# A gated network's gate and up products as seven half-size block products

## The chip, the core and the metric

The kernel runs on one NeuronCore of a Trainium2 chip. The core has a matrix engine (TensorE, "PE" in the profile; its weight loads are the row "PEld"), VectorE ("DVE"), ScalarE ("ACT"), GpSimd ("POOL") and SyncE ("SP"), which issues the transfers here. Each engine runs its own instructions in order and waits on semaphores for the others. The metric is the device time of one execution, in microseconds.

## What is computed

A sequence of 512 tokens of 1,024 values passes through a first block (a convolution and attention mixer, an attention to a memory, a feed-forward network with a short convolution) and then two layers of a second one. Each of the two layers has two gated networks, called here f10, f20 (layer 0) and f11, f21 (layer 1). Between f10 and f20 stands a pooling mixer, between f11 and f21 an attention with latent projections. The change touches the four gated networks alone.

```python
def swiglu(h, w_gate, w_up, w_down):
    return (jax.nn.silu(h @ w_gate) * (h @ w_up)) @ w_down
...
        h = rmsnorm_2(x, ffn1_norm[i])
        x = x + FFN_HALF * swiglu(h, ffn1_w_gate[i], ffn1_w_up[i], ffn1_w_down[i])
```

Here `w_gate` and `w_up` are 1024x2816 and `w_down` is 2816x1024. All is float32.

## The kernel before

**Numbers in two parts.** A float32 product is made of three matmuls in a rounded format (`fp32r`): every operand is split into a high part (rounded) and a low part (the rest), and `mm3` (L386 to L388) issues high by high, low by high and high by low. So each block of weights, once it has come by a transfer into a slot `raw`, is rounded into `wh` by ScalarE (`high`, L370), and VectorE subtracts that from the original into `wl` (`low`, L378). The stream x stands with its channels on the partitions, x[:, k, :] for the eight blocks k of 128 channels; its scaled halves are `hxh` (ScalarE, L515) and `hxl` (VectorE, L523).

**A unit** is one block of weights that makes one output tile of 128x512: eight row blocks of 128x128 (128x1024 in the profile) for gate and up, and for down eight, eight and six (the last is 128x768). A gated network has 22 tiles c. For each, `swiglu_tensor` (L1604) computes a gate tile and an up tile, 24 matmuls of 512 columns each. The first two units are run as a pair, k by k, since the last blocks of x come late. VectorE multiplies both tiles by the row factor `rs` of the norm (L1647, L1652), ScalarE takes the silu (L1637), GpSimd multiplies the two (L1703), ScalarE rounds the product into `hh` (L1640) and GpSimd makes its low part `hl` (L1705). All 22 are kept. Then each of the eight output tiles m takes three units of down, 66 matmuls, after which VectorE adds half of the result to x[:, m, :] (L1692), ScalarE splits and squares it for the next stage (L515, L447), VectorE makes `hxl` (L523), and GpSimd adds up the squares (L452).

**What sets the order** is the order in which the functions of each engine are written: nothing is scheduled by a tool. `swiglu_scalar` and `swiglu_vector` convert the weights two units ahead. `raw`, `wh` and `wl` have three slots each; a transfer into `raw` waits for the `low` three units earlier, a `high` for the matmuls three units earlier. The factor `rs` is made while the first tiles are computed: TensorE adds up the squares (L461), VectorE turns them into a mean square (L477), GpSimd takes the inverse root (L484), TensorE spreads it (L494) and ScalarE keeps it (L501). In f10 the spreading stands one unit later in TensorE's order than in the others (`LATE`).

## Time and profile before

| | |
|---|---|
| median of three runs | 2551.04 us (2550.62 to 2552.26) |
| profiled execution, span | 2550.8 us |
| TensorE (PE) busy | 2514.7 us, 99% |
| VectorE (DVE) busy | 1215.6 us, 48% |
| ScalarE (ACT) busy | 933.4 us, 37% |
| GpSimd (POOL) busy | 622.4 us, 24% |
| chain of work that ended last | 89% TensorE, 6% VectorE |

The page gives for each engine the time in which it had work. Matmuls overlap each other: a row's duration (0.39 us at 512 columns) is a latency, and the distance between the starts of two rows is what one costs. A row of VectorE that says "x2" covers two instructions, one after the other. What stands in brackets behind a row is how long the engine sat idle before it, and what ended that. "PEclk" is TensorE's granted clock as a share of its full 2.4 GHz.

### The profile page before, as it was taken

What the parts mean: (1) busy time and instruction counts of PE and PEld (TensorE: products, weight loads), DVE (VectorE), ACT (ScalarE), POOL (GpSimd) and SP (SyncE); (2) the same over time, 40 slices, a digit from 0 to 9 for tenths busy, and PEclk for the clock granted to TensorE, in tenths of its full rate; (3) what the DMA queues carried; (4) which work ended last, traced back from release to release, by engine and by line L of the source; (5) the groups of instructions that cost most, each with busy time, mean ns of one, the idle gap of its engine ahead of it and who ended that gap; (6) DMA issues with size and microseconds to landing.
All of it is one profiled execution on the core that took longest, in us unless ns stands there. A gap on an engine that the chain in (4) does not pass through costs nothing.

```text
span 2550.8 us, 28691 instructions
## 1 busy us (share of the span) xinstructions
PE 2514.7 (99%) x11642; PEld 2073.3 (81%) x11642; DVE 1215.6 (48%) x1607; ACT 933.4 (37%) x1371; POOL 622.4 (24%) x477
## 2 busy tenths in 40 slices
PE   8999999999999999999999999999999999999999
PEld 7777777888887888888888888888888888888887
DVE  5896655565635333335333333333336566433322
ACT  4486443444323332224333222332223554433221
POOL 3673403222203222101222101222101431322200
PEclk9999999999999999999999999999999999999999
DMA  5211312323232233332323332323332111333232
GB/s 171 71 46 58 105 44 67 107 92 98 93 99 81 90 93 98 98 97 75 107 92 96 96 99 88 108 93 97 92 100 87 42 50 58 94 96 95 93 99 93
DMA packets 66483, 227.26 MB, mean 89 GB/s; under 512 B 7216, under 2 KB 8752, under 8 KB 66352
## 3 DMA queue, kind: packets, MB, share of 16 engines
q1 hardware_dynamic: 66352, 225.44, 28.1%
q8 instruction: 92, 1.51, 0.3%
q14 instruction: 39, 0.32, 0.0%
HBM read 223.31 MB, written 2.10 MB: 88 GB/s over the span
## 4 chain that ended last, share of the span: by engine, by line
PE 89%; DVE 6%; ACT 2%; issue 1%; POOL 1%; DMA 0%; SPq 0%; DVEq 0%; ACTq 0%; POOLq 0%
PE main L386 19%; PE main L388 19%; PE main L387 19%; PE score L386 7%; PE score L388 6%; PE score L387 6%; PE out L386 3%; PE out L388 3%; PE out L387 3%; DVE wl L378 1%; DVE hxl L523 1%; DVE tmp L1347 1%; PE main L2055 1%; ACT wh L370 0%; PE turn L1027 0%
## 5 line engine op out<-in xcount | busy, mean ns | idle before, releaser
L378 DVE TENSOR_TENSOR wl<-raw,wh 128x1024 fp32r<-128x1024 f32 (+1 forms) x431 | 562.8, 1308 | 806.9 <-ACT wh L370 805.9
L370 ACT ACTIVATE wh<-raw 128x1024 fp32r<-128x1024 f32 (+1 forms) x431 | 439.9, 1024 | 635.7 <-PE main L388 473.2
L386 PE MATMUL main<-hxh,wh 128*128 128x512 f32 x1200 | 470.9, 392 | 8.2 <-DVE tmp L687 4.2
L388 PE MATMUL main<-hxh,wl 128*128 128x512 f32 x1200 | 467.9, 390 | 0.0
L387 PE MATMUL main<-hxl,wh 128*128 128x512 f32 x1200 | 467.8, 390 | 0.0
L386 PE MATMUL main<-hh,wh 128*128 128x512 f32 x880 | 342.4, 389 | 0.5 <-DVE wl L378 0.5
L387 PE MATMUL main<-hl,wh 128*128 128x512 f32 x880 | 342.3, 389 | 0.0
L388 PE MATMUL main<-hh,wl 128*128 128x512 f32 x880 | 342.3, 389 | 0.0
L452 POOL TENSOR_TENSOR acc<-acc,sq 128x512 f32<-128x512 f32 (+1 forms) x88 | 128.2, 1456 | 617.4 <-ACT sq L447 612.1
L386 PEld LDWEIGHTS main<-hxh,wh 128*128 128x128 f32 x1200 | 225.7, 188 | 60.1 <-DVE tmp L687 4.3
L388 PEld LDWEIGHTS main<-hxh,wl 128*128 128x128 f32 x1200 | 225.7, 188 | 47.5
L387 PEld LDWEIGHTS main<-hxl,wh 128*128 128x128 f32 x1200 | 225.7, 188 | 45.7
L1703 POOL TENSOR_TENSOR tmp<-tmp,tmp 128x512 f32<-128x512 f32 x88 | 113.5, 1289 | 607.7 <-DVE tmp L1652 562.8
L386 PE MATMUL score<-hxh,wh 128*128 128x512 f32 x656 | 257.3, 392 | 3.0 <-DVE wl L378 1.3
L388 PE MATMUL score<-hxh,wl 128*128 128x512 f32 x656 | 255.4, 389 | 0.0
L387 PE MATMUL score<-hxl,wh 128*128 128x512 f32 x656 | 255.3, 389 | 0.0
L386 PEld LDWEIGHTS main<-hh,wh 128*128 128x128 f32 x880 | 165.2, 188 | 35.0 <-issue 0.9
L387 PEld LDWEIGHTS main<-hl,wh 128*128 128x128 f32 x880 | 165.2, 188 | 34.4
L388 PEld LDWEIGHTS main<-hh,wl 128*128 128x128 f32 x880 | 165.2, 188 | 34.2
L1640 ACT ACTIVATE hh<-tmp 128x512 fp32r<-128x512 f32 x88 | 55.7, 633 | 317.8 <-POOL tmp L1703 317.8
L386 PEld LDWEIGHTS score<-hxh,wh 128*128 128x128 f32 x656 | 123.2, 188 | 32.3 <-DVE hxl L523 4.0
L388 PEld LDWEIGHTS score<-hxh,wl 128*128 128x128 f32 x656 | 123.1, 188 | 25.9
(434 smaller groups left out, 3412.5 us busy)
## 6 DMA issues: line engine op xcount, KB each, us to landing
raw<-in_wts SPq DMA_DIRECT2D x375, 512.0 KB, 3.5
raw<-in_wts SPq DMA_DIRECT2D x52, 384.0 KB, 3.0
x<-in_xT SPq DMA_DIRECT2D x4, 512.0 KB, 8.3
out<-x SPq DMA_DIRECT2D x8, 256.0 KB, 3.2
memx<-in_memT SPq DMA_DIRECT2D x1, 1024.0 KB, 9.6
raw<-in_wts SPq DMA_DIRECT2D x4, 256.0 KB, 2.6
band<-in_pool SPq DMA_DIRECT2D x1, 768.0 KB, 4.2
rope<-in_rope SPq DMA_DIRECT2D x1, 512.0 KB, 7.1
```

Of the source, the lines that this page charges most:

```text
L370: e.activation(wh[i % NCONV][:, 0:n], raw[i % NRAW][:, 0:n], ACT.Copy).then_inc(*sig.up("weight_high", ("high", i)))
L378: e.tensor_tensor(wl[i % NCONV][:, 0:n], raw[i % NRAW][:, 0:n], f(wh[i % NCONV][:, 0:n]), ALU.subtract) \
L386: e.matmul(o, ah, bh, start=start, stop=False)
L387: e.matmul(o, ah, bl, start=False, stop=False)
L388: return e.matmul(o, al, bh, start=False, stop=stop)
L452: e.tensor_tensor(acc[:, 0:n], acc[:, 0:n], sq_turn(nm).of(("sq", nm, k))[:, 0:n], ALU.add) \
L523: e.scalar_tensor_tensor(hxl[:, k, :], x[:, k, :], col(gain, k), f(hxh[:, k, :]), ALU.mult, ALU.subtract) \
L1347: e.scalar_tensor_tensor(s[:, :], y[:, m, :], col(gain, m), turnb.of(("rows", nm))[:, :], ALU.mult, ALU.mult) \
L1640: e.activation(hh[:, c, :], s[:, :], ACT.Copy).then_inc(*sig.up("h_high", ("hh", nm, c)))
L1703: e.tensor_tensor(s1[:, :], s1[:, :], s2[:, :], ALU.mult).then_inc(*sig.up("h_joined", ("joined", nm, c), ("free", (nm, "us", c))))
L2055: made = e.matmul(o[:, n * i:n * i + n], s[:, i * P:(i + 1) * P], ones[:, 2:4] if halves else ones[:, 0:1], start=True, stop=True)
```

## The change

Each gated network now runs in three rounds of 8, 8 and 6 tiles (`ROUNDS_OF`). In a round the tiles are computed and at once multiplied by their rows of down, for all eight m; the results are added into x three times over, each scaled by `rs` (so the up tiles are no longer scaled), and the part of the product that is kept (`bh`, `bl`) has eight tiles in place of 22.

Of the 22 tiles, 15 are computed as **blocks**: for a tile c, gate and up are taken as a matrix of 2x2 blocks (gate and up; upper and lower half of the 1,024 rows), and the stream as one of 2x2 blocks (upper and lower half of the rows; left and right 256 tokens). The eight products of blocks are replaced by seven, `UP_LEFT`, `UP_RIGHT`, `S1` to `S4` and `GATE_RIGHT`, some of them of sums of blocks. One product is 4 row blocks by 3 matmuls by 256 columns. The sums of weights (`sum_step`, four of 128x512 a tile) and the recombination (`up_left_vector` and the functions after it) are VectorE's; the sums of the stream (`turned_sums_vector`, four blocks k, once a network) are VectorE's too, with ScalarE rounding them. ScalarE copies three intermediate results out of the accumulating bank (`keep_scalar`). The other seven tiles stay plain: three at the start (`OPENING`) as before, and four (`HALVED`) in units of half the rows.

Conversions are now of halves (128x512), up to six halves ahead of TensorE, sums nine halves ahead, and during the down units four halves (two units) ahead. `raw`, `wh` and `wl` get a fourth slot in these networks. GpSimd makes only the low part of each gated tile (`h_low`); the multiplication goes to VectorE. The core of the diff:

```diff
+NHALF = 6
+HALF = 512
+AHEAD = 6
+Q = 256
...
+ROUNDS_OF = ((0, 8), (8, 8), (16, 6))
+BLOCKED = ("f10", "f20", "f11", "f21")
+OPENING = 3
+HALVED = (5, 10, 13, 18)
+UP_LEFT, UP_RIGHT, S4, GATE_RIGHT, S1, S2, S3 = 1, 2, 3, 4, 5, 6, 7
+GATE_TOP, GATE_LOW, UP_TOP, UP_LOW = 8, 9, 10, 11
+GATE, UP = 12, 13
+SUMS = (S1, S2, S3, S4)
+
...
+def tile_order(rnd):
+
+    c0, n = ROUNDS_OF[rnd]
+    order, behind = [], []
+    for c in range(c0, c0 + n):
+        if c < OPENING:
+            order += [(c, GATE), (c, UP)]
+        elif c in HALVED:
+            order += [(c, GATE_TOP), *behind[:1], (c, GATE_LOW), *behind[1:], (c, UP_TOP), (c, UP_LOW)]
+            behind = []
+        else:
+            order += [(c, UP_LEFT), (c, UP_RIGHT), *behind[:1], (c, S2), *behind[1:], (c, S1), (c, S3)]
+            behind = [(c, GATE_RIGHT), (c, S4)]
+    return order + behind
 
 
...
+            src, ready = weight_source(i)
+            e.wait_ge(*sig.at(ready))
+            for old in held[i]:
+                e.wait_ge(*sig.at(("unit", old)))
+            if half_at[i] >= NHALF:
+                e.wait_ge(*sig.at(area_ready[stage_name(units[i][0])]))
+            e.activation(halves_of(wh, i), src, ACT.Copy).then_inc(*sig.up("weight_high", ("high", i)))
...
+            if which == S1:
+                a, b, op = raw_half(r + 1, 0), raw_half(r + 1, 1), ALU.add
+            elif which == S2:
+                e.wait_ge(*sig.at(("summed", tile, S1)))
+                a, b, op = sums.of(("sum", tile, S1))[:, :], raw_half(r, 0), ALU.subtract
+            elif which == S3:
+                a, b, op = raw_half(r, 0), raw_half(r + 1, 0), ALU.subtract
+            else:
+                e.wait_ge(*sig.at(("summed", tile, S2)))
+                a, b, op = raw_half(r, 1), sums.of(("sum", tile, S2))[:, :], ALU.subtract
+            e.tensor_tensor(t[:, :], a, b, op).then_inc(*sig.up("weights_summed", ("summed", tile, which)))
+
...
+        def weights_ahead(step, e, i, halves=AHEAD):
+            for n in range(i + 1, reach(i, halves) + 1):
+                step(e, n)
...
+            first = which in (UP_LEFT, UP_RIGHT, S1)
+            e.wait_ge(*sig.at(("low", i)))
+            for k in range(4):
+                mh, ml, ready = moving(nm, which, k)
+                e.wait_ge(*sig.at(ready))
+                e.matmul(b[:, LEFT], h[:, k, :], mh, start=first and k == 0, stop=False, skip_group_check=not first)
+                e.matmul(b[:, LEFT], h[:, k, :], ml, start=False, stop=False, skip_group_check=not first)
+                made = e.matmul(b[:, LEFT], lo[:, k, :], mh, start=False, stop=k == 3, skip_group_check=not first)
+            made.then_inc(*sig.up("unit_done", ("unit", i)))
...
+        def down_step(e, nm, rnd, m, ks):
+            c0, n = ROUNDS_OF[rnd]
+            i = down_unit(nm, rnd, m)
+            b, (h, lo) = down_banks.of((nm, "bank", rnd, m)), weights_of(i)
+            e.wait_ge(*sig.at(("low", i)))
+            for k in ks:
+                e.wait_ge(*sig.at(("h", nm, c0 + k)))
+                made = mm3(e, b[:, :], (h[:, k, :], lo[:, k, :]), (bh[:, k, :], bl[:, k, :]), k == 0, k == n - 1)
+                if k == n - 1:
+                    made.then_inc(*sig.up("unit_done", ("unit", i)))
...
+                for m in range(2):
+                    _, old = down_banks.take((nm, "bank", rnd, m))
+                    e.wait_ge(*sig.at(old))
+                    down_step(e, nm, rnd, m, range(0, 2))
+                    block_product(e, nm, c0 + n - 1, (GATE_RIGHT, S4)[m])
+                for m in range(2):
+                    down_step(e, nm, rnd, m, range(2, n - 1))
+                for m in range(2):
+                    down_step(e, nm, rnd, m, range(n - 1, n))
+                for m in range(2, KC):
+                    _, old = down_banks.take((nm, "bank", rnd, m))
+                    e.wait_ge(*sig.at(old))
+                    down_step(e, nm, rnd, m, range(n))
+            wide.pass_over(2 * FT + (3 if nm == "f11" else 0))
...
+            e.activation(tsum[:, k, 3 * Q:4 * Q], x[:, k, LEFT], ACT.Copy, scale=col(GAIN[nm], k)).then_inc(*sig.up("left_kept", ("x left", nm, k)))
...
+            g, n = col(GAIN[nm], 4 + k), (slice(0, Q), slice(Q, 2 * Q), slice(2 * Q, 3 * Q), slice(3 * Q, 4 * Q))
+            e.wait_ge(*sig.at(("x left", nm, k)))
+            e.scalar_tensor_tensor(tsum[:, k, n[0]], x[:, k, RIGHT], col(GAIN[nm], k), tsum[:, k, n[3]], ALU.mult, ALU.subtract) \
+                .then_inc(*sig.up("turned_sum", ("t1 sum", nm, k)))
+            e.wait_ge(*sig.at(("t1 sum", nm, k)))
+            e.scalar_tensor_tensor(tsum[:, k, n[1]], x[:, 4 + k, RIGHT], g, tsum[:, k, n[0]], ALU.mult, ALU.subtract) \
+                .then_inc(*sig.up("turned_sum", ("t2 sum", nm, k)))
+            e.wait_ge(*sig.at(("t2 sum", nm, k)))
+            e.tensor_tensor(tsum[:, k, n[3]], tsum[:, k, n[1]], tsum[:, k, n[3]], ALU.subtract).then_inc(*sig.up("turned_sum"))
+            e.scalar_tensor_tensor(tsum[:, k, n[2]], x[:, 4 + k, LEFT], g, tsum[:, k, n[1]], ALU.mult, ALU.subtract) \
+                .then_inc(*sig.up("turned_sum", ("t sum", nm, k)))
...
+        def keep_scalar(e, nm, c, which):
+            t, old = kept_turn.take((nm, "kept", c, which))
+            e.wait_ge(*sig.at(old))
+            e.wait_ge(*sig.at(("unit", part_no[(nm, c), which])))
+            e.activation(t[:, :], a_banks.of((nm, "a", c))[:, LEFT], ACT.Copy).then_inc(*sig.up("sum_kept", ("kept", nm, c, which)))
...
+        def join_blocks(e, nm, c):
+            g = tile_turn.of((nm, "gate", c))
+            e.wait_ge(*sig.at(("silu", nm, c)))
+            e.wait_ge(*sig.at(("up", nm, c)))
+            e.tensor_tensor(g[:, :], g[:, :], tile_turn.of((nm, "up", c))[:, :], ALU.mult) \
+                .then_inc(*sig.up("blocks_joined", ("joined", nm, c), ("free", (nm, "up", c))))
...
+        def h_low(e, nm, c):
+            e.wait_ge(*sig.at(("hh", nm, c)))
+            e.tensor_tensor(bl[:, c % 8, :], tile_turn.of((nm, "gate", c))[:, :], f(bh[:, c % 8, :]), ALU.subtract) \
+                .then_inc(*sig.up("gated_low", ("h", nm, c), ("free", (nm, "gate", c))))
...
+                        weights_ahead(sum_weights, e, part_of(nm, c, which), AHEAD + 3)
+                        weights_ahead(low, e, part_of(nm, c, which))
+                    if rnd == 0 and s == 0:
+                        turned_sums_vector(e, nm, 0)
+                        turned_sums_vector(e, nm, 1)
+                        turned_low_vector(e, nm, 0)
+                    if rnd == 0 and s == (3 if nm in LATE else 2):
+                        mean_square(e, nm, 1.0 / D)
+                    if rnd == 0 and 2 <= s < 5:
+                        if s < 4:
+                            turned_sums_vector(e, nm, s)
+                        turned_low_vector(e, nm, s - 1)
+                    if rnd == 0 and s == 5:
+                        gate_plain_vector(e, nm, 0)
+                        gate_plain_vector(e, nm, 1)
+                    if rnd == 0 and s == 6:
+                        gate_plain_vector(e, nm, 2)
...
+                    weights_ahead(sum_weights, e, down_unit(nm, rnd, m), AHEAD)
+                    weights_ahead(low, e, down_unit(nm, rnd, m), 4)
+                    y, old = tile_turn.take((nm, "y", rnd, m))
+                    e.wait_ge(*sig.at(old))
+                    e.wait_ge(*sig.at(("unit", down_unit(nm, rnd, m))))
+                    e.scalar_tensor_tensor(y[:, :], down_banks.of((nm, "bank", rnd, m))[:, :], 0.5, rs[:, :], ALU.mult, ALU.mult) \
+                        .then_inc(*sig.up("y_scaled", ("y", nm, rnd, m), ("free", (nm, "bank", rnd, m)), *([("free", ("rs", nm))] if (rnd, m) == (2, KC - 1) else [])))
+                    e.wait_ge(*sig.at(("y", nm, rnd, m)))
+                    e.tensor_tensor(x[:, m, :], x[:, m, :], y[:, :], ALU.add) \
+                        .then_inc(*sig.up("x_even", ("x", nm, m) if rnd == 2 else ("x", nm, rnd, m), ("free", (nm, "y", rnd, m))))
+                    if rnd == 2 and next_nm:
+                        split_low(e, next_nm, m, next_gain)
+
...
-            for m in range(KC):
-                for p in range(3):
-                    low(e, u + 2 * FT + 3 * m + p + 2)
-                e.wait_ge(*sig.at(("unit", u + 2 * FT + 3 * m + 2)))
-                e.scalar_tensor_tensor(x[:, m, :], mainb.of(("y", nm, m))[:, :], 0.5, x[:, m, :], ALU.mult, ALU.add) \
-                    .then_inc(*sig.up("x_even", ("x", nm, m), ("free", ("y", nm, m))))
-                if next_nm:
-                    split_low(e, next_nm, m, next_gain)
...
-                s1, s2 = half_turn.of((nm, "gs", c)), half_turn.of((nm, "us", c))
-                e.wait_ge(*sig.at(("silu", nm, c)))
-                e.wait_ge(*sig.at(("up", nm, c)))
-                e.tensor_tensor(s1[:, :], s1[:, :], s2[:, :], ALU.mult).then_inc(*sig.up("h_joined", ("joined", nm, c), ("free", (nm, "us", c))))
-                e.wait_ge(*sig.at(("hh", nm, c)))
-                e.tensor_tensor(hl[:, c, :], s1[:, :], f(hh[:, c, :]), ALU.subtract).then_inc(*sig.up("h_low", ("h", nm, c), ("free", (nm, "gs", c))))
```

**TensorE, inside tile 8 of f20.** Before, the end of a gate unit and the start of the up unit (`main`, `score`, `out` are banks of results; behind the arrow stand the stream's part and the weights' part):

```order
L386 MATMUL score<-hxh_53,wh_59 128x512
L387 MATMUL score<-hxl_54,wh_59 128x512
L388 MATMUL score<-hxh_53,wl_62 128x512
L386 MATMUL score<-hxh_53,wh_60 128x512 [waits s_weight_low,s_half_scaled]
L387 MATMUL score<-hxl_54,wh_60 128x512
L388 MATMUL score<-hxh_53,wl_63 128x512
```

After, the end of `UP_RIGHT` and the start of `S2` (`th`, `tl` are the parts of the stream's sums):

```order
L1853 MATMUL out<-hxh_53,wh_60 128x256
L1854 MATMUL out<-hxl_54,wh_60 128x256
L1855 MATMUL out<-hxh_53,wl_63 128x256
L1853 MATMUL main<-th_144,wh_142 128x256 [waits s_weight_low,s_sum_kept]
L1854 MATMUL main<-tl_145,wh_142 128x256
L1855 MATMUL main<-th_144,wl_143 128x256
```

The matmuls have half as many columns, and `S2` waits for the copy that ScalarE makes of the bank after `UP_LEFT`.

**VectorE, output tiles of the last down round of f20.** Before, two output tiles m, three units of weights each:

```order
L1692 SCALAR_TENSOR_TENSOR x_49<-main,x_49 128x512 [waits s_unit_done]
L523 SCALAR_TENSOR_TENSOR hxl_54<-x_49,colsb_64,hxh_53 128x512 [waits s_x_high]
L378 TENSOR_TENSOR wl_63<-raw_57,wh_60 128x768 [waits s_weight_high]
L378 TENSOR_TENSOR wl_61<-raw_55,wh_58 128x1024 [waits s_weight_high]
L378 TENSOR_TENSOR wl_62<-raw_56,wh_59 128x1024 [waits s_weight_high]
L1692 SCALAR_TENSOR_TENSOR x_49<-main,x_49 128x512 [waits s_unit_done]
L523 SCALAR_TENSOR_TENSOR hxl_54<-x_49,colsb_64,hxh_53 128x512 [waits s_x_high]
L378 TENSOR_TENSOR wl_63<-raw_57,wh_60 128x768 [waits s_weight_high]
L378 TENSOR_TENSOR wl_61<-raw_55,wh_58 128x1024 [waits s_weight_high]
L378 TENSOR_TENSOR wl_62<-raw_56,wh_59 128x1024 [waits s_weight_high]
```

After, again two output tiles, one unit each:

```order
L2117 SCALAR_TENSOR_TENSOR tmp_77<-score,rs_69 128x512 [waits s_unit_done,s_gated_low]
L2120 TENSOR_TENSOR x_49<-x_49,tmp_77 128x512 [waits s_y_scaled]
L716 SCALAR_TENSOR_TENSOR hxl_54<-x_49,colsb_64,hxh_53 128x512 [waits s_x_high]
L526 TENSOR_TENSOR wl_62<-raw_57,wh_59 128x768 [waits s_weight_high]
L2117 SCALAR_TENSOR_TENSOR tmp_78<-out,rs_69 128x512 [waits s_unit_done,s_blocks_joined]
L2120 TENSOR_TENSOR x_49<-x_49,tmp_78 128x512 [waits s_y_scaled]
L716 SCALAR_TENSOR_TENSOR hxl_54<-x_49,colsb_64,hxh_53 128x512 [waits s_x_high]
L526 TENSOR_TENSOR wl_63<-raw_141,wh_60 128x768 [waits s_weight_high]
```

Per output tile one instruction came in ahead of the addition to x and two conversions went; between two tiles TensorE now has 18 matmuls and not 66.

**VectorE, opening of f10.** Before, from the last `hxl` to the first scaled tiles:

```order
L523 SCALAR_TENSOR_TENSOR hxl_54<-x_49,colsb_64,hxh_53 128x512 [waits s_x_high] x3
L378 TENSOR_TENSOR wl_62<-raw_56,wh_59 128x1024 [waits s_weight_high]
L378 TENSOR_TENSOR wl_63<-raw_57,wh_60 128x1024 [waits s_weight_high]
L378 TENSOR_TENSOR wl_61<-raw_55,wh_58 128x1024 [waits s_weight_high]
L378 TENSOR_TENSOR wl_62<-raw_56,wh_59 128x1024 [waits s_weight_high]
L477 TENSOR_SCALAR stat_51<-turn 128x4 [waits s_sums_done,s_m_divided]
L378 TENSOR_TENSOR wl_63<-raw_57,wh_60 128x1024 [waits s_weight_high]
L1647 TENSOR_TENSOR tmp_74<-score,rs_69 128x512 [waits s_x_even,s_unit_done,s_rows_kept]
L1652 TENSOR_TENSOR tmp_75<-out,rs_69 128x512 [waits s_x_odd,s_unit_done]
```

After, the twelve rows that end with the mean square (two sets of `tsum`, one `tl` and two conversions stand between the last `hxl` and these):

```order
L526 TENSOR_TENSOR wl_61<-raw_55,wh_58 128x1024 [waits s_weight_high]
L552 TENSOR_TENSOR sum_135<-raw_141 128x512 [waits s_unit_done,s_fetched3,s_fetched2]
L552 TENSOR_TENSOR sum_136<-sum_135,raw_57 128x512 [waits s_weights_summed]
L526 TENSOR_TENSOR wl_62<-raw_56,wh_59 128x1024 [waits s_weight_high]
L1943 SCALAR_TENSOR_TENSOR tsum_146<-x_49,colsb_64,tsum_146 128x256 [waits s_left_kept]
L1946 SCALAR_TENSOR_TENSOR tsum_146<-x_49,colsb_64,tsum_146 128x256 [waits s_turned_sum]
L1949 TENSOR_TENSOR tsum_146<-tsum_146 128x256 [waits s_turned_sum]
L1950 SCALAR_TENSOR_TENSOR tsum_146<-x_49,colsb_64,tsum_146 128x256
L1955 TENSOR_TENSOR tl_145<-tsum_146,th_144 128x1024 [waits s_turned_high]
L552 TENSOR_TENSOR sum_137<-raw_57,raw_141 128x512
L526 TENSOR_TENSOR wl_63<-raw_57,wh_60 128x512 [waits s_weight_high] x2
L670 TENSOR_SCALAR stat_51<-turn 128x4 [waits s_sums_done,s_m_divided]
```

The mean square was the fifth instruction after the last group of `hxl`, and now two conversions and sums of the stream and of the weights stand ahead of it.

## Rows read from the trace of the kernel before

**Rows 1.** Page, span; then part 1: busy us (share) xinstructions.

```profile
span 2550.8 us, 28691 instructions
PE 2514.7 (99%) x11642; PEld 2073.3 (81%) x11642; DVE 1215.6 (48%) x1607; ACT 933.4 (37%) x1371; POOL 622.4 (24%) x477
```

**Rows 2.** TensorE's longest wait (start us, us, engine, line), then its stretch (PEclk after POOL).

```profile
61.51 0.56 PE L386 MATMUL main<-hxh,wh 128*128 128x512 f32 x1 [4.21 <-DVE tmp L687]
60.00:73.00 13.00, 11.49 (x44) 9.34 (x45) 11.35 (x15) 3.87 (x5) 2.37 (x2) 0.87 0.26 83
```

**Rows 3.** Timeline, TensorE, 512 columns, first and last of 18 starts.

```profile
1100.10 0.39 PE L386 MATMUL main<-hh,wh 128*128 128x512 f32 x1
...
1103.95 0.39 PE L388 MATMUL main<-hh,wl 128*128 128x512 f32 x1
```

**Rows 4.** Timeline, TensorE, 256 columns, the first and the last of 22 starts.

```profile
129.36 0.28 PE L388 MATMUL main<-mnh,wl 128*128 128x256 f32 x1
...
131.87 0.28 PE L388 MATMUL main<-mnh,wl 128*128 128x256 f32 x1
```

**Rows 5.** Groups by line and form, VectorE: count | busy us, mean ns.

```profile
L1778 DVE SCALAR_TENSOR_TENSOR zl<-main,stat,zh 128x256 fp32r<-128x256 f32 x8 | 3.7, 479 | 1.9 <-ACT zh L1767 1.6
L734 DVE TENSOR_TENSOR mk_l<-main,mk_h 128x256 fp32r<-128x256 f32 x8 | 3.3, 415 | 0.5 <-ACT mk_h L729 0.5
L378 DVE TENSOR_TENSOR wl<-raw,wh 128x512 fp32r<-128x512 f32 x4 | 2.8, 690 | 6.7 <-ACT wh L370 6.7
```

**Rows 6.** Timeline, VectorE, two conversions in a row.

```profile
1173.32 0.69 DVE L1799 TENSOR_TENSOR band_l<-band,band_h 128x512 fp32r<-128x512 f32 x1 [3.47 <-ACT band_h L1791]
1173.93 0.68 DVE L378 TENSOR_TENSOR wl<-raw,wh 128x512 fp32r<-128x512 f32 x1
```

**Rows 7.** As rows 5, ScalarE's and GpSimd's groups.

```profile
L1640 ACT ACTIVATE hh<-tmp 128x512 fp32r<-128x512 f32 x88 | 55.7, 633 | 317.8 <-POOL tmp L1703 317.8
L1705 POOL TENSOR_TENSOR hl<-tmp,hh 128x512 fp32r<-128x512 f32 x88 | 114.4, 1300 | 65.4 <-ACT hh L1640 65.4
```

**Rows 8.** Timeline, VectorE and GpSimd together after 812 us.

```profile
815.19 6.69 DVE L378 TENSOR_TENSOR wl<-raw,wh 128x1024 fp32r<-128x1024 f32 x3
812.88 10.15 POOL L452 TENSOR_TENSOR acc<-acc,sq 128x512 f32<-128x512 f32 x5
```

**Rows 9.** Timeline, opening of f20, VectorE, GpSimd, TensorE.

```profile
1209.64 2.36 DVE L378 TENSOR_TENSOR wl<-raw,wh 128x1024 fp32r<-128x1024 f32 x2 [1.36 <-ACT wh L370]
1215.65 1.02 POOL L484 TENSOR_TENSOR stat<-stat,mhalf 128x4 f32<-128x4 f32 x1 [8.45 <-DVE stat L477]
1220.80 0.60 PE L494 MATMUL turn<-ident,stat 128*128 128x128 f32 x4
```

**Rows 10.** Timeline, last output tile but one of f11, VectorE, ScalarE, GpSimd.

```profile
1904.24 0.69 DVE L1692 SCALAR_TENSOR_TENSOR x<-main,x 128x512 f32<-128x512 f32 x1 [1.70 <-PE main L388]
1905.72 0.75 DVE L523 SCALAR_TENSOR_TENSOR hxl<-x,colsb,hxh 128x512 fp32r<-128x512 f32 x1 [0.79 <-ACT hxh L515]
1906.98 1.47 DVE L378 TENSOR_TENSOR wl<-raw,wh 128x768 fp32r<-128x768 f32 x1 [0.51 <-ACT wh L370]
1904.96 0.72 ACT L515 ACTIVATE hxh<-x,colsb 128x512 fp32r<-128x512 f32 x1 [3.69 <-DVE x L1692]
1905.59 0.62 ACT L447 ACTIVATE sq<-x 128x512 f32<-128x512 f32 x1
1906.11 0.83 ACT L370 ACTIVATE wh<-raw 128x768 fp32r<-128x768 f32 x1
1906.29 1.35 POOL L452 TENSOR_TENSOR acc<-acc,sq 128x512 f32<-128x512 f32 x1 [13.62 <-ACT sq L447]
```

**Rows 11.** Timeline, opening of f10, VectorE and TensorE.

```profile
829.60 0.16 DVE L477 TENSOR_SCALAR stat<-turn 128x4 f32<-128x4 f32 x1 [3.93 <-PE turn L461]
834.92 0.60 PE L494 MATMUL turn<-ident,stat 128*128 128x128 f32 x4
```

**Rows 12.** Timeline, VectorE, the last instruction of the program.

```profile
2548.10 0.69 DVE L1692 SCALAR_TENSOR_TENSOR x<-main,x 128x512 f32<-128x512 f32 x1 [13.06 <-PE main L388]
```

499 lines of the change are left out of this document (376 added, 123 removed).

## The prediction

> **What bounds the kernel now.** I read the page first: TensorE is busy 99% of the span [rows 1], and the longest thing it ever waits for takes 4.2 us [rows 2]. So a change gains what it takes from TensorE's stream and loses what it makes TensorE wait for, and both are counted one by one. Next I read the timeline of TensorE for the distance between starts, since its durations overlap. At 512 columns 17 starts lie in 3.85 us, 226.5 ns each [rows 3]; at 256 columns, in an earlier stage with the same three matmuls and a weight load for each, 21 starts lie in 2.51 us, 119.5 ns each [rows 4]. Half the columns is not half the cost: the difference is 107 ns for 256 columns, which leaves about 12.5 ns for each matmul whatever its size. VectorE is busy 48% over the whole span [rows 1], but it gets most of the new work, so its rows are read by stage.
>
> **What TensorE gains.** 60 tiles (15 in four networks) give up 48 matmuls of 512 columns each, 2,880 in all, and get 84 of 256 columns, 5,040. 2,880 x 0.2265 = 652.3 us, 5,040 x 0.1195 = 602.3 us [rows 3, 4]: a gain of **50.0 us**, 0.84 us a tile (10.87 before, 10.03 after). The down matmuls, 528 a network, stay as they are. The change does what it says: these numbers are the order's own.
>
> A rule of the Trainium skill can be held against this. What the rows show is 12 to 13 ns above the columns' time. The page "TensorE: Matmul & The Clock Gate" (section Back-to-back issue gap) gives columns / 2.4 GHz plus 2.5 ns; by it the change would gain 2,880 x 0.2158 - 5,040 x 0.1092 = 71 us, an estimate from the page. The rows stand against it at both sizes, by 10 ns.
>
> **Steady blocks: can VectorE keep up?** For a block tile it makes four sums and seven conversions of 128x512 and one multiplication, 0.69 us each, and five recombinations of 128x256 at 0.42 us [rows 5]: 12 x 0.69 + 5 x 0.42 = 10.4 us. Two in a row overlap: they start 0.61 us apart, not 0.69 [rows 6], so the tile is about 12 x 0.61 + 5 x 0.34 = 9.0, and 0.2 for steps that need the one before. GpSimd's low part (1.30 us [rows 7]) comes on top, as the two get in each other's way: three conversions of 1024 took 6.69 us beside GpSimd's additions, 2.23 each [rows 8], where two back to back elsewhere took 2.36, 1.2 each [rows 9]. That is 1.0 us for each GpSimd instruction. So 10.3 us stand against TensorE's 10.03. That overrun is small, blocks stand at most three in a row, weights are up to six halves (8.6 us) ahead, and a plain tile (four conversions, two scalings, 3.7 us and GpSimd's 1.0 against 10.87) pays it back. ScalarE has per tile seven conversions and two more of 0.63 and three short copies: under 7 us. I take **0** for the steady part; if the cover goes, see the third rival. The gated tile waits for fewer engines; a round's last one needs about 3.6 us of VectorE, ScalarE and GpSimd after its last product, and has 4.1 us or more of down matmuls ahead of it: 0, bound 1 us a network.
>
> **The last round of down: a new bound.** Before, each output tile m had 66 matmuls (15 us) in which to finish x and split it. Now, in the last round, it has 18: 18 x 0.2265 = 4.08 us. The chain on VectorE for one m can be read from the old one, in the network f11 [rows 10]. From the start of the addition to x (1904.24) over ScalarE's split (1904.96, 0.72), `hxl` (1905.72), ScalarE's square and next conversion (until 1906.94) and GpSimd's addition of squares (until 1907.64), VectorE's next weights are converted at 1906.98 + 1.47 = 1908.45: 4.21 us. All of that is queued in the same order in the new kernel, since VectorE stands at `hxl` until ScalarE has split x, and ScalarE's next `high` stands behind its square. Ahead of it comes the new scaling into y, 0.69 and 0.03 for the hand-over, less 0.08 of overlap. So VectorE needs **4.85 us per m where TensorE needs 4.08**, and it prepares the weights only two units ahead. Followed through: y(0) can start 0.3 after the end of unit 0, which I call 0. The second unit of the next stage is converted seven chains later, two of them with 128x1024 (0.27 longer): 0.3 + 5 x 4.85 + 2 x 5.12 = 34.8. Unhindered, TensorE would reach it at 0.68 (unit 1 ends three matmuls after unit 0) + 6 x 4.08 + 0.68 = 25.8. It waits 9 us. From f20 to f11 and from f11 to the latent stage that is 9.0 each; from f10 to the pooling mixer the next units are smaller, and its chain starts about 8 later, so 8. Together **26 us**; without GpSimd's part (4.4 a chain) 17, and that is the lower bound. f21 has no next stage: its chain is y, x and one conversion, 2.3 us, below 4.08.
>
> At the start of f11 and of the latent stage TensorE then stands still for over 4 us in one piece. The wait of 4.21 us in the trace was followed by a stretch with a mean granted clock of 0.87 [rows 2], that is, 3.4 of 13 us at 1.2 in place of 2.4 GHz, and half of that is lost: 1.7 us. Twice: **3.4 us** (0 to 7).
>
> **Opening of each network.** VectorE now makes the stream's sums there: per block k three of 0.48 and one of 0.42 us [rows 5], about 1.85 with the overlaps and hand-overs, and one conversion of 1.15. Two sets, a conversion, two units and two sums of weights stand ahead of the mean square. In f20, counted from the first conversion of the pair (1209.64 + 1.15): 3.7 + 1.15 + 1.15 + 1.25 + 1.15 gives 1219.2, and with GpSimd's 1.02 the root is there at 1220.4, just before TensorE spreads it (1220.80) [rows 9]. No wait, by 0.4 us. Then two more sets, three `tl`, six halves and three sums, 12.6 us, until the first gate tile is scaled at 1232.5 and its bank free; TensorE wants it at 1221.1 + 10.9 = 1232.0, and the third gate tile's bank 0.9 us later than it is wanted in turn. I take 1.5 to 2 us for f20 and f11 and 1 for f21. f10 is worse: GpSimd's seven additions there run beside VectorE [rows 8], and its mean square stands three conversions later. The sums of the stream last until about 827.5, and then come `tl` (828.7), the third gate unit's conversion (829.9), two sums (831.1), the next conversion (832.3), a set (834.2), `tl` (835.3), a sum and two halves (837.4); the mean square comes at 837.5, not 829.60, and TensorE, which spread it at 834.92 [rows 11], waits until 838.8. With 0.5 for the third gate unit, wanted at 829.4, 1.5 and 0.9 for the banks, 6 us. Together **11 us** (3 to 20).
>
> **The end.** The last x (0.69 us, [rows 12]) gets a scaling ahead of it: **0.7 us**.
>
> **The sum**: -50.0 + 26 + 3.4 + 11 + 0.7 = -8.9 us. The profiled span is 2550.8 us, 0.2 below the median; so 2551.0 - 8.9 = **2542 us**.
>
> **Rivals.** *The gain comes through nearly whole.* The last round's chain stays under 4.08 us, if ScalarE and GpSimd fall between VectorE's instructions otherwise than in [rows 10]; then the 26 and the 3.4 go: 2542 - 29.4 = 2513 us. For it: in the old kernel nothing waited there. Against it: 4.21 us is one unbroken chain of queue order. *The matmuls cost their columns alone.* If the 12.5 ns shrank with the size, 256 columns would take 107 and 512 214 ns: 2,880 x 0.214 - 5,040 x 0.107 = 77 us, so 27 more, 2515 us. Against it: [rows 4], four stretches of that stage alike. By the same page of the Trainium skill the fixed part would be 2.5 ns, which leads nearly there. *VectorE paces the blocks, and it is slower than before.* At whole durations it needs 10.4 + 1.0 = 11.4 us a block tile, 1.4 over TensorE. ScalarE's copy of `UP_LEFT`, for which `S2` waits, stands in its queue behind a conversion whose sum VectorE has yet to make, so some of that reaches TensorE long before the six halves are used up. If a third does, 0.5 us x 60 = 30, and the time is 2572 us. It decides the sign from 8.9 / 60 = 0.15 us a tile on. Against it: the plain tiles between.
>
> **How the numbers follow.** The forecast has a chance of 53%, its own range 2534 to 2553 (17 to 27 for the rounds' ends, 3 to 20 for the openings). The first rival 20% (2505 to 2522), the second 4%, the third 23% (2555 to 2590). From 2518 to 2566 about 8 in 10 are held: half of the first rival and of the second fall below, part of the third above. A measurement of this kernel can tell about 0.2% (5 us) from no change. The forecast's case gives 33 points to faster, 17 to same and 3 to slower; the first two rivals are faster; of the third 3 points are same, 20 slower: faster 57%, same 20%, slower 23%.
>
> **What would show it.** TensorE's starts 119 to 120 ns apart in the blocks; if 129, the gain is gone. In the last round of f20 and f11, VectorE's y operations 4.8 us apart, and TensorE waiting for `wl` up to 9 us in all there, once for over 4. In f10's opening a wait of some 3 us for the root. In the steady blocks no wait over 0.3 us; waits for kept copies or `wl` in every pair would be the third rival. The prediction is wrong in its main term if y stands 4.1 us apart.

## The result, and the profile after

The changed kernel takes 2575.55 us (median of four runs, 2575.05 to 2576.74), the kernel before 2551.65 us beside it. The ratio is 1.0095, with a 95% interval of 1.008 to 1.0109: about 24 us **slower**. I had forecast 2542 us, 9 faster, and the time lies above my range too. The profiled execution has a span of 2574.1 us, 23.3 more than before, so its rows can be set against the old ones directly.

The page, as [rows 1]:

```profile
span 2574.1 us, 34915 instructions
PE 2485.6 (97%) x13802; PEld 2142.7 (83%) x13802; DVE 1743.2 (68%) x2659; ACT 1126.4 (44%) x1915; POOL 529.4 (21%) x389
PE 82%; DVE 11%; ACT 3%; issue 3%; POOL 1%; DMA 1%; SPq 0%; DVEq 0%; ACTq 0%; POOLq 0%
```

TensorE is busy 29 us less than before, although the program is longer: it now stands still. In the chain of work that ended last it has 82% in place of 89%, and VectorE 11% in place of 6%. The view of TensorE's waits (engine, line, tile waited for: us in all, times, the longest) says where:

```profile
PE turn L687 <- POOL stat L677: 10.1, 3, 3.8
PE main L579 <- DVE wl L526: 8.7, 11, 3.5
PE main L579 <- DVE tmp L2117: 8.4, 3, 6.4
PE main L579 <- DVE x L3035: 7.7, 2, 7.4
PE main L579 <- DVE x L2209: 5.3, 1, 5.3
PE turn L662 <- ACT sq L640: 4.9, 1, 4.9
```

Here `stat L677` is the inverse root of a network's norm, `wl L526` a conversion of weights, `tmp L2117` the scaling of a down result into y, `x L3035` and `x L2209` the last additions to x of the attention and of the pooling mixer, and `sq L640` the squares of x ahead of the pooling mixer. None of these was over 0.9 us before. Over the whole program TensorE waits 83 us where it waited 32.

**What the blocks gave.** The distances that answer to [rows 3, 4], in a block tile of f11 (first and last of 20 starts):

```profile
1876.05 0.28 PE L1855 MATMUL main<-th,wl 128*128 128x256 f32 x1
...
1878.33 0.28 PE L1853 MATMUL main<-hxh,wh 128*128 128x256 f32 x1
```

19 distances in 2.28 us are 120.0 ns. The 512-column matmuls stand 226.5 ns apart as before, so the blocks give 2,880 x 0.2265 - 5,040 x 0.120 = 48 us where I had 50. The next lines are windows of f11: its second round from tile 8 to the first down unit, then a block tile alone (length, then busy us of TensorE, weight loads, VectorE, ScalarE, GpSimd; granted clock):

```profile
1707.26:1786.73 79.47, 79.47 (x577) 75.58 (x576) 65.43 (x106) 41.03 (x77) 10.09 (x6) 1.00 0.35 108
1871.49:1881.57 10.08, 10.08 (x86) 10.08 (x85) 8.97 (x17) 5.71 (x12) 0.00 (x0) 1.00 0.28 80
```

TensorE never stops, and the same stretch is 79.47 us long in all four networks. From tile 8 to the last down round nothing is lost anywhere.

**The last down round** (VectorE's and TensorE's timelines in f20; the brackets give the idle time ahead and what ended it):

```profile
1554.04 0.68 DVE L2117 SCALAR_TENSOR_TENSOR tmp<-main,rs 128x512 f32<-128x512 f32 x1
1554.76 0.69 DVE L2120 TENSOR_TENSOR x<-x,tmp 128x512 f32<-128x512 f32 x1
1556.24 0.75 DVE L716 SCALAR_TENSOR_TENSOR hxl<-x,colsb,hxh 128x512 fp32r<-128x512 f32 x1 [0.79 <-ACT hxh L708]
1557.49 1.46 DVE L526 TENSOR_TENSOR wl<-raw,wh 128x768 fp32r<-128x768 f32 x1 [0.50 <-ACT wh L517]
1558.88 0.68 DVE L2117 SCALAR_TENSOR_TENSOR tmp<-score,rs 128x512 f32<-128x512 f32 x1
...
1559.11 0.47 PE L579 MATMUL main<-bh,wh 128*128 128x512 f32 x1 [0.48 <-DVE wl L526]
1563.95 0.47 PE L579 MATMUL main<-bh,wh 128*128 128x512 f32 x1 [0.51 <-DVE wl L526]
...
1574.69 0.76 PE L579 MATMUL main<-hxh,wh 128*128 128x512 f32 x1 [6.41 <-DVE tmp L2117]
```

This is the chain of [rows 10] with the scaling ahead of it: 4.84 us from y to y. TensorE follows at that pace, and stands still 6.4 us before f11. Its waits of 0.5 us cost 4.84 - 4.08 = 0.76 each: the idle time that a row shows leaves out some 0.25 us of starting up again.

**The first pair of f21** (as [rows 9], another place):

```profile
2204.54 8.06 DVE L716 SCALAR_TENSOR_TENSOR hxl<-x,colsb,hxh 128x512 fp32r<-128x512 f32 x5 [0.33 <-ACT hxh L708]
2212.53 0.68 DVE L3035 TENSOR_TENSOR x<-main,x 128x512 f32<-128x512 f32 x1
...
2213.26 0.79 PE L579 MATMUL main<-hxh,wh 128*128 128x512 f32 x1 [7.35 <-DVE x L3035]
```

The attention's last x is added behind five `hxl`. It stood there before as well (VectorE of the kernel before, then all of TensorE's wait for that line):

```profile
2193.60 0.68 DVE L2612 TENSOR_TENSOR x<-main,x 128x512 f32<-128x512 f32 x1
...
PE main L386 <- DVE x L2612: 0.3, 1, 0.3
```

Now f21's first gate tile goes into the very bank that this addition reads out. f20 waits 5.3 us in the same way for the last pooled x.

**The opening of f20** (as [rows 9]):

```profile
1225.43 1.22 DVE L526 TENSOR_TENSOR wl<-raw,wh 128x1024 fp32r<-128x1024 f32 x1
1230.56 0.69 DVE L552 TENSOR_TENSOR sum<-raw 128x512 f32<-128x512 f32 x1 [3.91 <-DMA raw<-in_wts]
1231.97 1.22 DVE L526 TENSOR_TENSOR wl<-raw,wh 128x1024 fp32r<-128x1024 f32 x1
1233.10 0.15 DVE L670 TENSOR_SCALAR stat<-turn 128x4 f32<-128x4 f32 x1
...
1226.68 0.81 SPq L483 DMA_DIRECT2D raw<-in_wts  x2
...
1234.68 1.09 PE L687 MATMUL turn<-ident,stat 128*128 128x128 f32 x4 [3.75 <-POOL stat L677]
```

The first sum of weights needs a block that SyncE could issue only at 1226.68, when the conversion ahead had emptied its slot. VectorE stands still in front of that sum for 3.9 us, with the mean square queued behind it. The same happens in f21; in f11 the rotation of the slots is another, and the block is there in time.

### The profile page after: what moved, and what is told of

Read it like the earlier page. It is cut to its first block, busy times and chain, and to the rows that moved or that the text cites. A ratio compares the mean times of both kernels' runs of the same rounds, so it can differ in the third digit from the quotient of the medians.

```text
span 2574.1 us, 34915 instructions
## 1 busy us (share of the span) xinstructions
PE 2485.6 (97%) x13802; PEld 2142.7 (83%) x13802; DVE 1743.2 (68%) x2659; ACT 1126.4 (44%) x1915; POOL 529.4 (21%) x389
## 4 chain that ended last, share of the span: by engine, by line
PE 82%; DVE 11%; ACT 3%; issue 3%; POOL 1%; DMA 1%; SPq 0%; DVEq 0%; ACTq 0%; POOLq 0%
PE main L579 12%; PE main L580 11%; PE main L581 11%; PE main L1855 6%; PE main L1854 6%; PE main L1853 6%; PE score L579 5%; PE score L580 4%; PE score L581 4%; DVE wl L526 2%; PE out L579 2%; PE out L580 2%; PE out L581 2%; PE score L1853 2%; PE score L1855 2%
## 5 line engine op out<-in xcount | busy, mean ns | idle before, releaser
L526 DVE TENSOR_TENSOR wl<-raw,wh 128x512 fp32r<-128x512 f32 (+2 forms) x523 | 551.5, 1059 | 287.0 <-ACT wh L517 285.5
L517 ACT ACTIVATE wh<-raw 128x512 fp32r<-128x512 f32 (+2 forms) x523 | 425.4, 829 | 468.7 <-PE main L581 272.1
L581 PE MATMUL main<-hxh,wl 128*128 128x512 f32 x808 | 317.6, 393 | 0.0
L1855 PE MATMUL main<-th,wl 128*128 128x256 f32 x840 | 237.7, 283 | 0.0
L1854 PE MATMUL main<-tl,wh 128*128 128x256 f32 x840 | 237.7, 283 | 0.0
L1853 PE MATMUL main<-th,wh 128*128 128x256 f32 x840 | 237.6, 283 | 0.0
L526 DVE TENSOR_TENSOR wl<-sum,wh 128x512 fp32r<-128x512 f32 x240 | 171.4, 727 | 25.3 <-ACT wh L517 22.2
L1853 PEld LDWEIGHTS main<-th,wh 128*128 128x128 f32 x840 | 161.2, 192 | 1.1
L1854 PEld LDWEIGHTS main<-tl,wh 128*128 128x128 f32 x840 | 161.2, 192 | 1.1
L1855 PEld LDWEIGHTS main<-th,wl 128*128 128x128 f32 x840 | 161.2, 192 | 0.0
```

What stands on the lines that cost most here:

```text
L517: e.activation(halves_of(wh, i), src, ACT.Copy).then_inc(*sig.up("weight_high", ("high", i)))
L526: e.tensor_tensor(halves_of(wl, i), src, f(halves_of(wh, i)), ALU.subtract) \
L581: return e.matmul(o, al, bh, start=False, stop=stop)
L1853: e.matmul(b[:, LEFT], h[:, k, :], mh, start=first and k == 0, stop=False, skip_group_check=not first)
L1854: e.matmul(b[:, LEFT], h[:, k, :], ml, start=False, stop=False, skip_group_check=not first)
L1855: made = e.matmul(b[:, LEFT], lo[:, k, :], mh, start=False, stop=k == 3, skip_group_check=not first)
```

## The experiments

All start from the changed kernel, or from it with edits named there. Every time is a median of repeated runs, set against the changed kernel's 2575.55 us.

### Turning the rings of result banks

A ring hands out its banks in turn, and `pass_over(n)` makes it skip n places. The edit changes which bank is next at the border between two stages, and nothing else.

```diff
-            wide.pass_over(2 * FT + (3 if nm == "f11" else 0))
+            wide.pass_over(2 * FT + {"f10": 5, "f11": 3}.get(nm, 0))
+            if nm == "f10":
+                a_banks.pass_over(1)
+            else:
+                c_banks.pass_over(1)
```

> The changed kernel with the rings of result banks turned by one place at the borders, so that the first pair of f20, f11 and f21 stands in banks that were read out long before; no instruction is added or moved. In the changed kernel TensorE waits 5.3 us at f20's first pair for x L2209 (the last pooled x) and 7.4 us at f21's for x L3035 (the last x of the attention), each followed by 6.8 us at the half clock. Theory A (the bank is the cause): both waits shrink to under 0.6 us, 12.2 us gained; at f11's first pair the wait of 6.4 us falls only by about 0.6, since the conversion of the second unit ends there at nearly the same time; and with no long wait the two stretches at the half clock go, 3.4 us each: 2575.5 - 12.8 - 6.8 = 2556 us. If the clock falls all the same: 2563. Rival B (TensorE is held back there by something behind the bank, the split of x or the weights): the waits get another name and the time stays at 2573 to 2576.

Measured: 2556.56 us. Both waits are gone: in the view of TensorE's waits no line stands for f20's first pair, and f21's reads

```profile
PE main L579 <- DVE wl L526: 0.5, 1, 0.5
```

Theory A. That its 2556 us was met to half a microsecond is luck in part, since the nine runs of this version lie between 2555.0 and 2562.3 us. 19 us came from which bank a tile stands in, with no instruction added, removed or moved.

The bank had a share at f11 too. TensorE's 6.4 us ahead of f11's first pair stood against `tmp L2117`, the scaling that reads out the bank which that pair takes. With the rings turned, TensorE waits 0.8 us at the pair's first matmul and 4.0 at its second unit, both for weights (f20's last round and f11's start, one view):

```profile
PE score L579 <- DVE wl L526: 4.6, 2, 4.0
PE main L579 <- DVE wl L526: 1.7, 3, 0.8
```

So 1.6 us of the 6.4 were the bank's, and the other 4.8 the late weights that I had forecast there.

### The mean square ahead of the weights

```diff
+                    if rnd == 0 and s == (3 if nm in LATE else 2):
+                        mean_square(e, nm, 1.0 / D)
+                    if rnd == 0 and 2 <= s < 5:
+                        if s < 4:
+                            turned_sums_vector(e, nm, s)
+                        turned_low_vector(e, nm, s - 1)
                     if which:
                         weights_ahead(sum_weights, e, part_of(nm, c, which), AHEAD + 3)
                         weights_ahead(low, e, part_of(nm, c, which))
...
-                    if rnd == 0 and s == (3 if nm in LATE else 2):
-                        mean_square(e, nm, 1.0 / D)
...
```

> The changed kernel with VectorE's mean square and the sums of the stream moved ahead of the sums and conversions of weights of the same step in each opening; in f20 and f21 VectorE stands still 3.9 us there, in front of a sum whose transfer has not landed, with the mean square behind it. Theory A: TensorE's waits for the root (3.0 in f10, 3.8 in f20, 3.7 in f21) go; in f20 and f21 the idle time is filled, so that the first scaled gate tiles come 3 us earlier too and the waits for their banks stay at about 1 to 2 us; in f10 nothing was idle, and the 3.0 come back as a wait for the bank. With the two stretches at the half clock behind the waits (1.7 us each): 2575.5 - 7.5 - 3.4 = 2565 us. Rival B (VectorE's work up to the gate tiles is the bound and not its order): the waits move to the banks (tmp L2017) one for one, and 2572 to 2576 us remain.

Measured: 2567.95 us, 7.6 less; 10.9 were expected. TensorE's waits in the opening of f20 (first fence: changed kernel; second: this one):

```profile
PE turn L687 <- POOL stat L677: 3.8, 1, 3.8
PE main L1853 <- DVE tmp L2017: 1.3, 1, 1.3
PE out L1853 <- DVE tmp L2017: 0.7, 1, 0.7
```

```profile
PE main L1853 <- DVE tmp L2017: 2.5, 1, 2.5
```

The root is in time. Of the 5.8 us of waits, 2.5 stay as a wait for the bank of a gate tile that is not yet scaled. In f10, where nothing stood idle, 2.8 for the root became 1.1 and the bank's wait grew from 0.9 to 2.7, one for one, as I had expected. Both theories have a part: A in f20 and f21, B in f10.

### The conversion behind x in the last down round

```diff
+                    behind = rnd == 2 and next_nm and m < KC - 1
+                    if not behind:
+                        weights_ahead(sum_weights, e, down_unit(nm, rnd, m), AHEAD)
+                        weights_ahead(low, e, down_unit(nm, rnd, m), 4)
...
                     e.tensor_tensor(x[:, m, :], x[:, m, :], y[:, :], ALU.add) \
...
+                    if behind:
+                        weights_ahead(sum_weights, e, down_unit(nm, rnd, m), AHEAD)
+                        weights_ahead(low, e, down_unit(nm, rnd, m), 4)
                     if rnd == 2 and next_nm:
                         split_low(e, next_nm, m, next_gain)
```

> The changed kernel with one reordering on VectorE in the last down round, for m = 0 to 6: scaling y, addition to x, then the conversion of weights two units ahead, then the low part of the stream, so that VectorE converts while ScalarE splits x (before, the conversion stood ahead of y and VectorE stood still behind x). Theory A (the queue order makes 4.84 us per output tile): VectorE's tile falls to about 3.6 us, the four waits of 0.65 us in each of three last rounds go (7.9 us), and of the waits at the start of what follows (4.9 pooling, 6.4 f11, 4.8 latent) about 2.5, 2.5 and 2 stay, 9 us less; the stretches at the half clock behind them (3.4 us lost at each of f11 and the latent stage, 5.1 at the pooling mixer against 3.4 in the kernel before) shorten by up to 8.5 us: 2550 us, or 2559 if the clock stays as it is. Rival B (VectorE's work per tile is the bound, in whatever order, or ScalarE's chain split, square, conversion is): y stays 4.6 to 4.9 us apart, 2573 to 2576 us.

Measured: 2553.29 us, 22 less and level with the kernel before (ratio 1.0002, 0.9992 to 1.0011), between the 2550 and the 2559 that theory A gave with and without the clock. VectorE in f20's last round:

```profile
1543.26 0.69 DVE L2119 SCALAR_TENSOR_TENSOR tmp<-main,rs 128x512 f32<-128x512 f32 x1 [0.61 <-PE main L581]
1543.99 0.69 DVE L2122 TENSOR_TENSOR x<-x,tmp 128x512 f32<-128x512 f32 x1
1544.60 0.95 DVE L526 TENSOR_TENSOR wl<-raw,wh 128x768 fp32r<-128x768 f32 x1
1545.47 0.75 DVE L716 SCALAR_TENSOR_TENSOR hxl<-x,colsb,hxh 128x512 fp32r<-128x512 f32 x1
1547.34 0.69 DVE L2119 SCALAR_TENSOR_TENSOR tmp<-score,rs 128x512 f32<-128x512 f32 x1 [1.12 <-PE score L581]
```

From y to y it is now 4.08 us, TensorE's pace, and VectorE is the one that waits. It needs 3.0 us a tile: the order filled ScalarE's 0.79, and the conversion takes 0.95 and not 1.46 us: in the changed kernel GpSimd's addition of squares ran beside it (1556.80 to 1558.14 us), here it has ended (1543.80 us) or not yet begun (1546.04 us). Theory A. Some 6 us of the waits that the last rounds had brought stay: 2.0 at the pooling mixer, 2.8 at f11, 1.5 at the latent stage, less the 0.7 of before.

### All three

> The three edits together: banks turned, mean square and stream sums first, conversion behind x in the last down rounds. Theory A (three separate causes, which add up, and f11's first pair now waits neither for the bank nor long for the second unit): 2575.5 - 19.6 - 10.9 - 25.5 = 2519.5 us, and 2538 if the clock gives nothing back; faster than the kernel before in both cases. Rival B (what is taken away at one place comes back at the next, since VectorE's work as a whole is the bound): 2555 us or more.

Measured: 2525.14 us, ratio to the kernel before 0.9891 (0.9876 to 0.9906). **This version beats both kernels**, by 1.1% and 2.0%. The three gains were 19.0, 7.6 and 22.3; together they gave 50.4. The causes are separate and add up. (Theory A's 2519.5 us was 6 too low, since it took the gain of the second edit as forecast and not as measured, and more from the third.) The waits for the root are down from 10.1 to 1.1 us. What is left of the openings are the gate tiles' banks, 7.9 us in all (I had written 8.4 in the next expectations):

```profile
PE main L1853 <- DVE tmp L2021: 5.8, 4, 2.7
PE score L1853 <- DVE tmp L2021: 1.4, 2, 0.7
PE out L1853 <- DVE tmp L2021: 0.7, 1, 0.7
```

### Twelve of fifteen blocks undone

```diff
-HALVED = (5, 10, 13, 18)
+HALVED = (3, 4, 5, 6, 8, 9, 10, 11, 12, 13, 14, 16, 17, 18, 19, 20)
```

> The changed kernel with its three rounds and its openings, but only tiles 7, 15 and 21 of a network as blocks; the other twelve of the fifteen are plain tiles in halves, 48 in four networks. By the rows of the changed kernel a plain tile takes 48 x 0.2267 = 10.88 us and a block tile 84 x 0.120 = 10.08 us of TensorE, 38 us for 48 tiles. Theory A (in the steady blocks TensorE alone sets the time, and every microsecond that blocks save there is in the measured time): 2575.5 + 38 = 2614 us; since no sum of weights stands in an opening any more, the two waits for the root behind a sum's transfer (3.8 and 3.7) and their clock (1.7 each) may go too, which gives 2603. Rival B (VectorE's work for blocks costs the steady part something, say 0.3 us a tile, as my third rival had it): 14 us less of a loss, 2589 to 2600.

Measured: 2594.45 us, 19 more, in the range of rival B. The waits show why it is not B. What the openings gave back was more than I had put in. The waits for the root are down to one of 0.9 us (9.2 us less), and no line is left for the gate tiles' banks (5.1 us less). 38 - 9.2 - 5.1 is 24, and of the stretches at the half clock those in the openings of f20 and f21 (3.4 us each, 1.7 lost each) are gone: 20.

Where the blocks are computed their gain can be read directly. These are windows of f11, from the last matmul of the first down round to the first of the second, in the changed kernel and in this one; between them five blocks have become plain tiles:

```profile
1707.04:1786.73 79.69, 79.69 (x578) 75.77 (x577) 65.43 (x106) 41.03 (x77) 10.09 (x6) 1.00 0.35 108
```

```profile
1716.28:1799.86 83.58, 83.58 (x398) 70.44 (x397) 39.57 (x54) 28.51 (x47) 9.70 (x7) 1.00 0.28 99
```

That is 0.78 us a tile, where the rows of TensorE gave 0.80. The stretches of the third round (58.7 us, now 61.8, four blocks fewer) say the same, and so do those of the other three networks. Rival B's 0.3 us a tile is not there. So 48 blocks bring 38 us where they are computed, and nearly half of it went at once into the openings.

### Matmuls in place of the waits

```diff
         def block_tensor(e, nm):
+            if nm != "f10":
+                keep_warm(e, (nm, "first pair"), {"f20": 22, "f11": 26, "f21": 30}[nm])
```

> The changed kernel with 22, 26 and 30 extra matmuls on TensorE (128x256, 0.216 us each by an earlier stage's rows) ahead of the first pair of f20, f11 and f21, into a bank that nobody reads: they stand in the waits of 5.3, 6.4 and 7.4 us, and are shorter than these (4.8, 5.6, 6.5 us), so the first pairs start when they did. Theory A (the granted clock falls because TensorE stands still there): the three stretches of 6.8 us at half clock that follow these waits go, 3.4 us each: 2575.5 - 10.2 = 2565 us, with the waits otherwise as they were. Rival B (the clock falls there whatever TensorE does, or such matmuls don't hold it): 2575 to 2577 us.

Measured: 2583.79 us, slower. My edit was mis-sized: an unrounded float32 matmul takes two rows of 0.216 us, not one, so the fill outlasted the waits. Halved:

```diff
-{"f20": 22, "f11": 26, "f21": 30}
+{"f20": 11, "f11": 13, "f21": 15}
```

> As the run before with extra matmuls in the changed kernel, which took 0.43 us each there (two passes, so twice what I had read from the rows) and so outlasted the waits by 3.8 to 5 us; now 11, 13 and 15 of them, 4.7, 5.6 and 6.5 us in waits of 5.6, 6.8 and 7.7 us from matmul to matmul. Theory A (the clock falls because TensorE stands still): the stretches at half clock that began 1203.8, 1572.5 and 2210.8 us after the start go. Part of each lay inside the wait; TensorE worked in 5.0, 4.6 and 4.3 us of them at half speed, so half of 13.9 us is gained: 2575.5 - 7.0 = 2568.5 us. Rival B (it falls there whatever TensorE does): 2575 to 2577 us. In the first version these three stretches were gone, which speaks for A, but the time could not show it.

Measured: 2570.61 us, 4.9 less, where A said 7.0 and B none. The start of f11 as a window, first the changed kernel, then this one (the granted clock is the number behind GpSimd's count):

```profile
1573.00:1579.00 6.00, 4.31 (x10) 3.47 (x11) 4.46 (x5) 2.19 (x3) 1.33 (x1) 0.50 0.32 90
```

```profile
1573.00:1579.00 6.00, 6.00 (x28) 4.99 (x27) 2.27 (x2) 1.84 (x3) 1.34 (x1) 1.00 0.46 139
```

The clock fell to 1.2 GHz where TensorE had stood still for 6.4 us, and stayed at 2.4 GHz where it was given idle work. All three stretches went. That is theory A for these three places. For the 2 us that are missing there is one candidate that I did not test: ahead of f10, where the two programs are alike, the stretches at the half clock sum to 6.8 us in the changed kernel's trace and to 17 us in this one, and half of TensorE's work in them is 3.4 and 7.3 us.

### Gate tiles scaled earlier

On top of all three edits. The first part, for both runs (the scalings now stand ahead of the weights of their step):

```diff
-                    if rnd == 0 and s == (5 if nm in LATE else 4):
+                    if rnd == 0 and s == 3 + late:
                         keep_rows(e, nm)
...
+                    if rnd == 0 and s == 4 + late:
+                        gate_plain_vector(e, nm, 0)
+                        gate_plain_vector(e, nm, 1)
+                    if rnd == 0 and s == 5 + late:
+                        gate_plain_vector(e, nm, 2)
```

The second part, for the first run alone, here for silu; the high part and VectorE's product move by the same step:

```diff
-                    if rnd == 0 and 6 <= s < 9:
+                    if rnd == 0 and 5 + late <= s < 8 + late:
                         silu_scalar(e, nm, s - 5 - late)
```

> The kernel with all three edits (2525.1 us), and in each opening the rows kept one step earlier on ScalarE, the first three gate tiles scaled ahead of the weights' sums and conversions on VectorE one step earlier, and silu, product and high part one step earlier (in f10 gate tile scaling only moves ahead of the weights). In that kernel TensorE still waits for these scalings (tmp L2021) 8.4 us in all. Theory A (what is late is the place in VectorE's queue): about 1 us of these waits stays, 2525.1 - 7.5 = 2517.6 us. Rival B (the openings have too much work for VectorE, and the weights or the stream's sums become late in turn): new waits for wl or tl take the place, 2523 to 2527 us.

> The kernel with all three edits (2525.1 us), and of the fourth edit only the rows kept one step earlier on ScalarE and the first gate tiles scaled ahead of the weights on VectorE; silu, product and high part stay where they were. With the whole fourth edit (2524.2 us) the waits for the scaling fell from 8.4 to 2.2 us, but TensorE waited 3.1 us for kept copies of UP_LEFT and 1.1 for the root of f10 instead, and the stretch from tile 3 to tile 8 of f10 and f20 grew from 95.9 and 96.5 to 98.7 and 98.9 us. Theory A (ScalarE stood at the high part of the gated tiles, waiting for VectorE's product, with the kept copy behind it, because those were moved up): without that move the stretches are 95.9 us again and the gain at tile 3 stays (2.4 us each in f10 and f20, 0.8 in f21): 2525.1 - 5.5 = 2519.6 us. Rival B (VectorE has too much to do in the opening, in whatever order): the kept copies or the banks of the up tiles are late again, 2523 to 2526 us.

Measured: 2524.20 us with the whole edit, 2522.82 with its first part (2525.14 without). TensorE's waits in the blocks of the first, then of the second:

```profile
PE main L1853 <- ACT kept L1965: 3.1, 3, 2.3
PE score L1853 <- DVE tmp L2021: 2.0, 1, 2.0
```

```profile
PE score L1853 <- DVE tmp L2021: 2.0, 1, 2.0
PE score L1853 <- DVE tmp L2028: 1.2, 1, 1.2
PE main L1853 <- ACT kept L1965: 1.1, 2, 0.8
```

The waits for the scaling fell from 7.9 to 2.2 us, but the block of tile 3, which starts sooner, waits for the next late thing. Without the move of silu and high part the waits for kept copies fall from 3.1 to 1.1 us, so A's mechanism is there, but 2.3 us and not 5.5 are gained. Mostly B: what leaves one place of the openings comes back at the next. That VectorE's work as a whole is what bounds them is the likely reading, and not shown; how much a better order could still give was not tried.

### Two sums of every block tile made twice

```diff
+            if which in (S1, S3):
+                e.tensor_tensor(t[:, :], a, b, op).then_inc(*sig.up("made_twice", ("made twice", tile, which)))
+                e.wait_ge(*sig.at(("made twice", tile, which)))
             e.tensor_tensor(t[:, :], a, b, op).then_inc(*sig.up("weights_summed", ("summed", tile, which)))
```

> The kernel with all three edits (2525.1 us), with two of the four sums of weights of every block tile made twice on VectorE, the second after the first has ended: 0.69 + 0.1 us each, 1.5 us a block tile, so that VectorE, busy 8.97 of a block tile's 10.08 us in the changed kernel, needs about 10.45 us, somewhat more than the 10.3 that I had put against TensorE's 10.03. Theory A (halves ahead and the plain tiles between take up an overrun of 0.4 us a tile): 2525 to 2530 us. Rival B (the kept copy behind a conversion hands every overrun on, as the third rival of the prediction says): 0.2 to 0.4 us x 60, 2537 to 2549 us, and waits for kept copies or wl in every pair of blocks.

Measured: 2539.62 us, 14.5 more, B's size. But the place is another. The second round of f11 took 79.8 us from tile 8 to down in place of 79.47, the third from tile 16 to down 58.95 in place of 58.45. Summed over the four networks these two stretches lost 3.2 us, and tiles 3 to 7 three more. Most of the rest is in the openings ahead of tile 3, and in the clock behind them:

```profile
PE main L1856 <- DVE tmp L2024: 12.2, 4, 4.2
PE main L1856 <- ACT kept L1968: 2.9, 6, 0.8
```

The first line is again the scaling of the first gate tiles (13.3 us with its two smaller rows, 7.9 before the edit), the second the kept copies. The overrun in the steady blocks was larger than the 0.4 us that I had written, where I had left out GpSimd: a doubled sum takes 0.71 us from start to start, so a block tile needs 8.97 + 1.4 = 10.4 us of VectorE, and 1.1 more where GpSimd works beside it, against TensorE's 10.08. It costs about 0.1 us a tile all the same, as A had it. The plain tiles take it up: over the second round of f11 VectorE is busy for 71.4 of the 79.8 us.

In the openings there is no such cover, and what VectorE is given more turns up in TensorE's waits.

## Why the prediction was wrong, point by point

| term | forecast | measured |
|---|---|---|
| matmuls of the blocks | -50.0 | -48 |
| steady blocks | 0 | 0 |
| last down rounds and what follows them (1.6 of it f11's bank) | +26 | +21 |
| openings: root and gate tiles' banks | +11 | +15 |
| first pairs of f20 and f21: banks of the stage before | 0 | +12.7 |
| clock | +3.4 | +10.8 |
| end | +0.7 | +0.8 |
| sum | -8.9 | +12 |

The span says +23.3. Of the 11 us that the table leaves, some 7 may be the starting up again behind 29 more waits, an estimate from the 0.25 us of the last round; the other 4 are spread over small rows that I did not pursue. The waits are those of the view above (for the last rounds 12 waits of 0.5, 4.9 - 0.7, 6.4, and 1.3 + 3.5 at the latent stage), the clock is half of the time in which TensorE worked at 1.2 GHz, 24.0 us lost against 13.2, and the end is the time from the start of the last matmul to the end of the program, 4.0 us against 3.2.

**The gain of TensorE** was right: 120.0 ns for 256 columns where [rows 4] said 119.5. The Trainium skill's page "TensorE: Matmul & The Clock Gate" (section Back-to-back issue gap) gives 109.2 by its formula, which it calls the gap of a matmul by itself, and 131 ns as sustained spacing at 512 columns; this trace shows 120.0 and 226.5, and the measurement decides.

**The steady blocks** were right. VectorE needs 8.97 us in a block tile without GpSimd's part, forecast 9.0. GpSimd's instruction costs it 1.1 us, forecast 1.0 (two rows of f11; elsewhere such a conversion takes 0.69):

```profile
1755.42 1.81 POOL L2029 TENSOR_TENSOR bl<-tmp,bh 128x512 fp32r<-128x512 f32 x1 [13.73 <-ACT bh L1971]
1755.99 1.79 DVE L526 TENSOR_TENSOR wl<-raw,wh 128x512 fp32r<-128x512 f32 x1
```

The Trainium skill's "GPSIMD Engine Reference" (section Specifications) has GpSimd contend for SBUF with VectorE instructions that have two SBUF inputs; `wl` has two, and the trace agrees, at 1.1 us.

**The last down rounds** were right in mechanism, place and nearly in size: 4.84 us from y to y where I had 4.85; before f11 2.0 + 6.4 us where I had 9.0 (1.6 of it the bank's, which I had not seen), before the latent stage 2.0 + 4.8 where I had 9.0, at the pooling mixer 2.0 + 4.2 where I had 8. The experiment that reorders them took away all but some 6 us of these waits, and with the clock and the starting up behind them 22 us of time.

**The step that failed** is one that is missing from the sum, the banks of the stage before, put at nothing without a reason: the two waits for them are 12.7 us. What is late next was asked of VectorE's queue and of the weights, never of the banks. The change brings four new rings of banks (`a_banks`, `b_banks`, `c_banks`, `down_banks`), and the program's order prints `main` for three different banks. I took it that a first pair finds its banks free, as it always had. Turning the rings gave back 19 of the 24 us, with what it changed of the clock and at f11; with that edit alone the kernel is 0.2% slower than the one before.

**The openings** had about the right total for the wrong reasons. f10 came as forecast (2.8 us for the root, "some 3"; 1.6 for banks). For f20 I had the mean square at 1219.2 and no wait, and it came at 1233.10. Some 8 us of that is the later start of the network, 2.5 the half clock behind its first wait, and 3.9 the idle time in front of the sum. The step was "3.7 + 1.15 + 1.15 + 1.25 + 1.15": it takes the sums of weights by their durations and leaves out their transfer, which SyncE could issue only when the slot was empty.

**The clock** was the second term that failed: 3.4 us in the sum, 10.8 measured. It was sized by one wait and counted only at the two that I had foreseen; there it lost 2.3 us each where I had 1.7. One such wait of 4.2 us both kernels have. Of the others in the changed kernel each of 3.5 us and more has a stretch at the half clock with it, 3.4 to 10.2 us long, seven in all, against one of 6.8 us at the same places before. So most waits that I missed cost more than themselves.

**The rivals.** The first fell with the 4.84 us from y to y, the second with the 120.0 ns. The third rival forecast 2572 us, and the time was 2575; that the number is near is chance, as the steady blocks, which were to lose it, lose nothing. A rival about where the banks come from was not among them.

## What to carry to other kernels

When a change brings new rings of buffers or banks, write down for each border between stages which buffer the next stage takes first and which instruction frees it, and look that instruction up in the queue of its engine; a place that costs nothing today is free only as long as the rotation is. Follow the operands of each new instruction back to their transfer, and that to the slot it waits for, before its duration is counted as its cost. And where an engine waits for another in the middle of its own tile, put work that is due anyway into that gap: one reordering of this kind was worth 22 us here, nearly as much as the whole change had lost.

## What the runs showed of the hardware

In three waits of 5.3, 6.4 and 7.4 us the half clock followed TensorE's standing still and not the stage: with idle matmuls in the waits the granted clock stayed at 2.4 GHz in all three places. A long wait is not the only thing that a stretch at the half clock can follow. In the kernel before, TensorE was granted 1.2 GHz from 1171.1 to 1177.9 us, behind a wait of 0.7 us and a row of 128x1 matmuls; what caused that was not tested. A float32 matmul of 256 columns that is not in the rounded format costs 0.43 us (two rows of 0.216), 3.6 times the 0.120 of the rounded one. The same conversion of 128x768 took 1.46 us beside GpSimd's addition of squares and 0.95 with GpSimd idle.
